# The last three experts of a hybrid decoder step keep their tokens' rows on chip and norm them there; all other rows are normed while those experts run

## Chip, cores and metric

One core of one Trainium2 chip. The metric is the device time of one execution in microseconds (us); the kernel before took 1431.51 us, the median of 3 runs (1427.43 to 1433.01).

## What is computed

One step of a one-layer trunk over 1024 prompt tokens and 32 sample tokens of width 1024, all in float32: RMSNorm, a projection, two mixers (an RWKV-7 recurrence and sliding-window attention), an output projection, and then the part that the change is in:

```python
x = x + (mixed @ prm['w_out']).astype(x.dtype)
h2 = rmsnorm(x, prm['norm_ffn_g'])
x = x + hier_moe(h2.reshape(Bn * T, D), prm).reshape(Bn, T, D).astype(x.dtype)
...
y = rmsnorm(x, norm_final_g)      # for the prompt and for the sample tokens
```

`hier_moe` sends each token to one of 4 groups (top 1) and in it to 2 of the group's 4 experts (top 2). An expert is `(silu(x @ w_gate) * (x @ w_up)) @ w_down` with 1024 x 512 and 512 x 1024 matrices, and its rows are added with the token's weight. A token's two experts always lie in one group, so experts of different groups share no token. RMSNorm multiplies a row by one over the root of its mean square (plus 1e-6) and by the gains.

## The kernel before, in words

Everything up to the routing fills the first 930 us of the profile. Then `h2` (the normed rows) and `x` lie in DRAM as `h2_dram` and `x_dram`, the second with 160 spare rows behind the 1056 tokens, and the 16 experts run one after the other, each over 160 slots: 128 in part A (`xgA`) and 32 in part B (`xgB`). A loop over rounds stands around them (7 at most, as many as the fullest expert needs); here one round runs and six are skipped, each with a few register and branch instructions.

An expert at position e takes these steps. GpSimd (POOL) gathers its rows from `h2_dram` with two indirect DMAs. TensorE (PE) turns them (`turn`, lines 1158 to 1172); ScalarE (ACT) and VectorE (DVE) copy the turned rows out of PSUM (`turned`). PE forms gate and up in four blocks of columns f = 0 to 3 (`gate_up`, 1174 to 1185) in two PSUM banks; ACT takes the SiLU of a block (`silu`, 1563), DVE multiplies (`product`, 2048), and block f of PE waits until the product of block f - 2 is done. `down` (1187 to 1204) writes 128 x 512 to banks 5 and 6 and the 32 slots of part B, cut into four column quarters on 4 x 32 partitions, to bank 7. ACT and DVE weight the three pieces (`rows_out`, 1570 and 2053), and POOL adds the rows to `x_dram` with two indirect accumulating DMAs (`scatter`, 2173). PE's order is turn(e), down(e - 1), gate_up(e).

SyncE (SP) issues all plain DMAs from one queue, in program order. The three matrices of an expert (2 MB each) go to one of two buffers; those of position e are asked for when down(e - 2) is done (line 552).

After the last expert's scatter has landed and the rounds are left, the tail runs: SP loads `x_dram` back into `X2` (nine tiles: eight of 128 tokens and one of 32; five DMAs in four pieces, `XL`, lines 557 to 560), ACT squares and sums each tile and takes the root (1598, 1600), DVE takes the reciprocal and multiplies by it and by the gains (2113, 2114) into `yo`, and SP stores the tiles (564).

Of the kernel before, what the change touches and what calls it, by code (L numbers as in the profile page):

```python
# [6 lines left out]
I32 = mybir.dt.int32  # L7
# [32 lines left out]
ROUNDS = -(-TOK // CAP)  # L40
LV = 6
# [24 lines left out]
sv_out sv_in st_in pool sr_ok sy_out sy_in st_out ys_ps ys_ok  # L66
# [3 lines left out]
fin """  # L70


def constants():
# [33 lines left out]
    return {"c_table": table.astype(np.float32), "c_level": level, "c_bias": bias.astype(np.float32),  # L107
# [9 lines left out]
def program(nc, i, o):  # L117

    ctx = ExitStack()
    with ctx:  # L120
# [136 lines left out]
        rt_ = {}  # L257
        for n, k in (("lg", 180), ("ga", 36), ("gb", 36), ("ohg", 36), ("prod", 144), ("leg", 36), ("oh1", 36), ("oh2", 36), ("OH1", 144), ("OH2", 144),
                     ("OHs", 144), ("tot", 144), ("rank", 144), ("cnt", 16), ("rk", 18), ("m", 9), ("gw", 9), ("m1", 9), ("m2", 9),
                     ("den", 9), ("mc", 1), ("nr", 1), ("cmp", 1), ("t16", 16), ("u16", 16)):  # L260
            rt_[n] = part(R0, k)
            R0 += k
# [11 lines left out]
        STEPS = 7  # L274
# [27 lines left out]
        assert R0 + 2 * NE <= ARENA  # L302

        yo = part(E0, NTT * D).rearrange("p (t d) -> p t d", t=NTT)
        x_quarters = x_dram.rearrange("r (j c) -> (r j) c", j=TQ)

# [68 lines left out]
        def _(sp):  # L375
# [163 lines left out]
            sp.wait_ge(s["h2o0"], 32 * 5)  # L539
            sp.wait_ge(s["h2o1"], 32 * 4)  # L540
            for a in range(2):
                load_expert(a, a)
            sp.wait_ge(s["n_rounds"], 1)
            rounds = sp.value_load(nround[0:1, 0:1], min_val=1, max_val=ROUNDS)
            with sp.Fori(0, ROUNDS) as r:  # L545
                with sp.If(rounds > r):  # L546
                    with sp.If(r > 0):
                        for a in range(2):
                            load_expert(a, a)
# [7 lines left out]
            x_rows = x_dram[0:SEQ].rearrange("(t p) d -> p t d", p=P)  # L557
            for n, (a, b) in enumerate(XL):
                sp.dma_start(X2[:, a:b, :], x_rows[:, a:b]).then_inc(s[f"x{n}"], 16)  # L559
            sp.dma_start(X2[0:NS, NT, :], x_dram[SEQ:TOK]).then_inc(s["x3"], 16)  # L560
            for t in range(NTT):
                sp.wait_ge(s["fin"], t + 1)
                dst = o["y_prompt"][0, t * P:(t + 1) * P, :] if t < NT else o["y_sample"].rearrange("b t d -> (b t) d")
# [1673 lines left out]
```

## Time and profile before

| | us |
|---|---|
| median of 3 runs | 1431.51 (1427.43 to 1433.01) |
| the profiled execution, its own time | 1429.26 |
| span of that execution, first to last instruction | 1427.5 |
| PE busy (matmuls) | 1297.9, 91% of the span |
| DVE, ACT, POOL busy | 460.1, 357.8, 279.7 |
| moved by DMA | 173.61 MB, 122 GB/s over the span |

The span is what the rows below divide; the execution's own time is 1.8 us longer, and its median over runs another 2.3 us. Times in the rows are microseconds from the first instruction. A busy share near 1 of PE does not say that it works at its peak.

### The profile page before, as it was taken

To read this page: it belongs to the slowest core of one execution; us is meant where nothing else is said; L and a number is where in the kernel's file an instruction comes from. 1 tells how busy PE (TensorE), PEld (TensorE's weight loads), DVE (VectorE), ACT (ScalarE), POOL (GpSimd) and SP (SyncE) were. 2 spreads that over 40 slices of the span, in tenths; PEclk is the share of its full clock that TensorE was granted. 3 is DMA by queue.
4 is the path that set the end of the run, shared out by engine and by line. 5 is a ranking of instruction groups with operands and counts; after the bars stand their busy time and mean duration, and the time that the engine had idled before them with its cause. 6 is when DMAs were issued, how large, how long until landed. Compare 5 with 4: busy or idle time off the path is not lost. (4 is left out here: it accounts for less than half of the span.)

```text
span 1427.5 us, 28133 instructions
## 1 busy us (share of the span) xinstructions
PE 1297.9 (91%) x12448; PEld 941.6 (66%) x12448; DVE 460.1 (32%) x879; ACT 357.8 (25%) x722; POOL 279.7 (20%) x159
## 2 busy tenths in 40 slices
PE   6999999988998988989799999489999999999990
PEld 4666656555666978777644454377887788788860
DVE  4103544366645555645342111511011111111113
ACT  4103444434442442333231112011011011101103
POOL 0000000011001999991000000011211211121010
PEclk9999999999999999999999999579999999999995
DMA  7312000100103000022303111917888788778817
GB/s 216 86 44 63 15 14 3 30 29 23 30 19 58 4 5 4 3 48 66 108 16 140 59 59 63 353 60 232 273 287 294 230 274 300 261 254 281 279 20 262
DMA packets 95259, 173.61 MB, mean 122 GB/s; under 512 B 19096, under 2 KB 41043, under 8 KB 94756
## 3 DMA queue, kind: packets, MB, share of 16 engines
q1 hardware_dynamic: 87476, 151.12, 31.3%
q0 software_dynamic: 7680, 20.98, 6.2%
q8 instruction: 82, 1.34, 0.4%
q14 instruction: 21, 0.17, 0.0%
HBM read 146.65 MB, written 26.44 MB: 121 GB/s over the span
## 5 line engine op out<-in xcount | busy, mean ns | idle before, releaser
L620 PE MATMUL ps<-arena 128*128 128x355 f32 x960 | 297.6, 466 | 1.9 <-issue 1.8
L1183 PEld LDWEIGHTS ps<-arena 128*128 128x128 f32 x2048 | 280.2, 191 | 6.9 <-issue 6.9
L1183 PE MATMUL ps<-arena 128*128 128x160 f32 x2048 | 284.1, 301 | 0.6 <-DVE arena L2046 0.6
L620 PEld LDWEIGHTS ps<-arena 128*128 128x128 f32 x960 | 179.7, 190 | 110.9 <-issue 13.4
L1083 PE MATMUL ps<-arena 128*128 128x512 f32 (+1 forms) x288 | 130.6, 603 | 0.7 <-DVE arena L1867 0.7
L860 PEld LDWEIGHTS ps<-arena 64*64 64x64 f32 x3584 | 110.3, 136 | 10.6 <-issue 6.1
L1197 PE MATMUL ps<-arena 128*128 128x512 f32 x256 | 114.1, 599 | 0.7 <-DVE arena L2051 0.7
L860 PE MATMUL ps<-arena 64*64 64x64 f32 x3584 | 114.3, 219 | 0.0
L2186 POOL DMA_INDIRECT arena<-h_dram,idxA x16 | 16.1, 1006 | 486.6 <-DVE idxB L2081 282.4
L2051 DVE TENSOR_TENSOR arena<-arena,ps 128x160 f32<-128x160 f32 x64 | 20.6, 321 | 265.5 <-ACT arena L1568 265.5
L1568 ACT ACTIVATE arena<-ps 128x160 f32<-128x160 f32 x64 | 19.5, 304 | 337.3 <-PE ps L1183 337.3
L1083 PEld LDWEIGHTS ps<-arena 128*128 128x128 f32 (+1 forms) x288 | 51.4, 183 | 66.5 <-issue 64.8
L2129 POOL TENSOR_TENSOR arena<-arena 128x1024 f32<-128x1024 f32 x4 | 11.4, 2854 | 377.8 <-DVE arena L1690 377.8
L1197 PEld LDWEIGHTS ps<-arena 128*128 128x128 f32 x256 | 47.3, 190 | 55.2 <-issue 53.6
L1256 ACT COPY arena<-ps 128x355 f32<-128x355 f32 x60 | 27.1, 452 | 175.0 <-PE ps L620 175.0
L2182 POOL DMA_INDIRECT x_dram<-arena,rowA x16 | 25.6, 1597 | 168.0 <-DVE arena L2060 168.0
L2058 DVE TENSOR_SCALAR arena<-ps,arena 128x512 f32<-128x512 f32 x16 | 12.0, 751 | 106.8 <-PE ps L1197 106.8
L2150 POOL TENSOR_TENSOR arena<-arena 128x1024 f32<-128x1024 f32 (+4 forms) x40 | 41.0, 1024 | 2.8
L1489 ACT COPY arena<-ps 128x512 f32<-128x512 f32 x40 | 23.4, 586 | 63.6 <-PE ps L860 63.6
L1719 DVE SCALAR_TENSOR_TENSOR arena<-ps,arena 128x1024 f32<-128x1024 f32 (+1 forms) x16 | 18.5, 1158 | 62.5 <-PE ps L699 62.5
L1805 DVE COPY_PREDICATED arena<-level,ps 128x512 f32<-128x512 uint8 x32 | 23.5, 734 | 41.6 <-PE ps L860 41.6
L1550 ACT COPY arena<-ps 128x512 f32<-128x512 f32 (+1 forms) x18 | 9.2, 553 | 109.3 <-PE ps L1144 109.3
(344 smaller groups left out, 1642.0 us busy)
## 6 DMA issues: line engine op xcount, KB each, us to landing
arena<-in_w_exp_gate SPq DMA_DIRECT2D x16, 2048.0 KB, 12.5
arena<-in_w_exp_up SPq DMA_DIRECT2D x16, 2048.0 KB, 17.4
arena<-in_w_exp_down SPq DMA_DIRECT2D x16, 2048.0 KB, 21.8
arena<-in_w_in SPq DMA_DIRECT2D x16, 512.0 KB, 3.9
arena<-in_x_prompt SPq DMA_DIRECT2D x9, 512.0 KB, 3.8
h_dram<-arena SPq DMA_DIRECT2D x8, 512.0 KB, 2.6
x_dram<-arena SPq DMA_DIRECT2D x8, 512.0 KB, 3.6
out_y_prompt<-arena SPq DMA_DIRECT2D x8, 512.0 KB, 5.9
```

The lines of the kernel that those rows point to most:

```text
L620: last = pe.matmul(ps[:, q % 2, 0:m], wr[:, n % 3, k, :], hT[:, k, a:a + m], start=(k == 0), stop=(k == KB - 1))
L860: last = pe.matmul(ps[row(e), 4 * b + bank, h * CH:(h + 1) * CH], lhs(e, h), rhs(e, h), start=True, stop=True)
L1083: return pe.matmul(ps[0:n, 4 * (t % 2) + hf, :], MX[:, b, t * P:t * P + n], wo[b][:, hf * 512:(hf + 1) * 512], start=(b == 0), stop=(b == 7))
L1183: last = pe.matmul(ps[:, 3 + f % 2, n * CAP:(n + 1) * CAP], w[a][:, k, f * P:(f + 1) * P], xgT[:, a, k, :], start=(k == 0), stop=(k == KB ...
L1197: last = pe.matmul(ps[:, 5 + n, :], eact[:, a, k, 0:P], edown[a][:, k, n * 512:(n + 1) * 512], start=(k == 0), stop=(k == 3))
L1256: act.copy(pT[:, pos, a:a + m], ps[:, q % 2, 0:m]).then_inc(s["p_ok"], 1)
L1489: act.copy(U[:, b].rearrange("p h t -> p (h t)"), ps[:, 4 * b, :]).then_inc(s["ru_ok"], 1)
L1568: act.activation(egl[:, f % 2, :], ps[:, 3 + f % 2, 0:CAP], ACT.Silu).then_inc(s["sl_ok"], 1)
L1805: dve.copy_predicated(TL[:, b], lm(lv, 0, 2 * JB), ps[:, 4 * b + 1, :].rearrange("p (h t) -> p h t", t=CH)).then_inc(s["rx_ok"], 1)
L2051: dve.tensor_tensor(eact[:, a, f, :], egl[:, f % 2, :], ps[:, 3 + f % 2, CAP:2 * CAP], ALU.mult).then_inc(s["ac_ok"], 1)
L2150: link(pool.tensor_tensor(stm[:, :, 0:m], stm[:, :, 0:m], stm[:, :, m:2 * m], ALU.add))
L2182: pool.indirect_dma_start(dst, bass.IndirectOffsetOnAxis(rows[:, e:e + 1], 0), src[:, e % 2, :], None, compute_op=ALU.add).then_inc(s[f"ys ...
```

## The change

The experts run in another order (`EO`): the first 13 positions hold experts 0 to 6, 8 to 10 and 12 to 14; the last three hold 7, 11 and 15, which lie in three groups and share no token. The first 13 add their rows to `x_dram` as before. For each of the last three, POOL gathers the `x_dram` rows of its slots (`xsA`, `xsB`), DVE adds the expert's weighted output to them on chip, and they are normed in slot order. Part B's mean square is the sum of four partitions' sums; PE forms it by a matmul with a 0/1 matrix `same` that takes the place of `strict` in the table. POOL then scatters the finished rows to both outputs by plain indirect DMAs with a bound on the index: one to `y_prompt` and one to `y_sample` for each of parts A and B, and indices outside an output are dropped.

Once the first 13 scatters have landed, the whole of `x_dram` is loaded into `X2`, squared on ACT between the SiLUs of position 14 and normed in place on DVE before and during position 15, and stored. The rows of the last three experts' tokens are written twice, the second time by the scatters, which wait until the stores have landed. The old tail is gone.

In the diff, `EO[e]` in place of `e` as an index of rows, weights and matrices, a renaming of two semaphores and the declarations are left out, as is what serves rounds after the first.

```diff
+LAST = 3
+EO = [e for e in range(NE) if e % EPG < EPG - 1 or e < EPG] + [e for e in range(EPG, NE) if e % EPG == EPG - 1]
+ACC = NE - LAST
...
+        gq = part(S0, TD)
+        xsA = [part(S0 + TD, D), xgA[:, 0, :], xgA[:, 1, :]]
+        YST = [32 * len(range(k, ACC, 2)) for k in range(2)]
+        FA, FD, FP = 22, 7, LAST
...
 # SP
+            sp.dma_start(x_dram[TOK:TOK + P, :], X2[:, 0, :]).then_inc(s["h2o0"], 16)
+            sp.dma_start(x_dram[TOK + P:, :], X2[0:XB, 1, :]).then_inc(s["h2o1"], 16)
...
-                    with sp.Fori(1, NE // 2) as q:
-                        for a in range(2):
-                            sp.wait_ge(s["ya_ps"], 3 * (NE * r + 2 * q + a) - 3)
-                            load_expert(2 * q + a, a)
+                    for e in range(2, NE):
+                        sp.wait_ge(s["ya_ps"], 3 * (NE * r + e) - 3)
+                        load_expert(EO[e], e % 2)
+                        if e == 2:
+                            sp.dma_start(same, i["c_same"]).then_inc(s["x0"], 16)
+                            for j in range(TQ):
+                                sp.dma_start(gq[j * XB:(j + 1) * XB, :], i["norm_final_g"][None, j * TD:(j + 1) * TD].to_broadcast([XB, TD])).then_inc(s["x0"], 16)
+                    for k in range(2):
+                        sp.wait_ge(s[f"yst{k}"], YST[k] * (r + 1))
+                        alone(sp)
+                    for n, (a, b) in enumerate(XL):
+                        if n == 0:
+                            sp.wait_ge(s["x0"], X_IN[0] + 80 * (r + 1) + 16 * r)
+                        sp.dma_start(X2[:, a:b, :], x_rows[:, a:b]).then_inc(s[f"x{n}"], 16)
+                    sp.dma_start(X2[0:NS, NT, :], x_dram[SEQ:TOK]).then_inc(s["x3"], 16)
+                    for t in range(NTT):
+                        sp.wait_ge(s["fin"], NTT * r + t + 1)
+                        dst = y_rows[t * P:(t + 1) * P, :] if t < NT else ys_rows
+                        sp.dma_start(dst, X2[0:toks(t), t, :]).then_inc(s[f"h2o{t % 2}"], 16)
...
 # PE
+                    def quarter_sums(k):
+                        pe.wait_ge(s["fn_act"], FA * r + (1, 15, 21)[k])
+                        pe.matmul(ps[:, 7, TD:TD + 1], same, stat[:, (50, 35, 47)[k]:(51, 36, 48)[k]], start=True, stop=True).then_inc(s["fn_pe"], 1)
+                    turn(g0 + NE - 2, 0, False)
+                    down(g0 + NE - 3, 1, False)
+                    gate_up(g0 + NE - 2, 0, False)
+                    pe.wait_ge(s["x0"], X_IN[0] + 96 * (r + 1))
+                    quarter_sums(0)
+                    turn(g0 + NE - 1, 1, False)
+                    pe.wait_ge(s["fn_act"], FA * r + 13)
+                    down(g0 + NE - 2, 0, False)
+                    gate_up(g0 + NE - 1, 1, False)
+                    quarter_sums(1)
+                    pe.wait_ge(s["fn_act"], FA * r + 17)
+                    down(g0 + NE - 1, 1, False)
+                    quarter_sums(2)
...
 # ACT: silu(g, a, first, between) calls between(f) after the SiLU of block f
+                    def rows(t):
+                        for k, (a, b) in enumerate(XL):
+                            if t == a:
+                                act.wait_ge(s[f"x{k}"], X_IN[k] + ((96, 16, 16, 32)[k]) * (r + 1))
+                        n = toks(t)
+                        if t:
+                            act.wait_ge(s["fn_act"], fa + 2 + t)
+                        square(eyA[0:n, 0, :], X2[0:n, t, :], t).then_inc(s["fn_act"], 1)
+                    def before_last(f):
+                        if f == 0:
+                            act.wait_ge(s["yo_dve"], 2 * (g0 + ACC) + 2)
+                            act.wait_ge(s["yst1"], YST[1] * (r + 1))
+                            square(eyB[:, 1, :], xsB[:, 0, :], 50).then_inc(s["fn_act"], 1)
+                            square(eyA[:, 1, :], xsA[0], 9).then_inc(s["fn_act"], 1)
+                            rows(0)
+                        elif f < 3:
+                            for t in range(3 * f - 2, 3 * f + 1):
+                                rows(t)
+                        else:
+                            rows(7)
+                            rows(8)
+                            act.wait_ge(s["fn_act"], fa + 11)
+                            root(10, stat[:, 0:10]).then_inc(s["fn_act"], 1)
+                            act.wait_ge(s["fn_pe"], FP * r + 1)
+                            root(30, ps[:, 7, TD:TD + 1]).then_inc(s["fn_act"], 1)
+                    def at_last(f):
+                        if f == 0:
+                            act.wait_ge(s["yo_dve"], 2 * (g0 + ACC + 1) + 2)
+                            act.wait_ge(s["fn_dve"], FD * r + 2)
+                            square(eyA[:, 0, :], xsA[1], 32).then_inc(s["fn_act"], 1)
+                            square(eyB[:, 0, :], xsB[:, 1, :], 35).then_inc(s["fn_act"], 1)
+                        elif f == 3:
+                            act.wait_ge(s["fn_act"], fa + 14)
+                            root(33, stat[:, 32:33]).then_inc(s["fn_act"], 1)
+                            act.wait_ge(s["fn_pe"], FP * r + 2)
+                            root(36, ps[:, 7, TD:TD + 1]).then_inc(s["fn_act"], 1)
...
 # DVE: sums(k, h) adds piece h of expert k of the last three; bulk(t) norms tile t of X2 in place; own and own_tail norm xsA and xsB
+                    dve.wait_ge(s["fn_act"], fa + 13)
+                    dve.reciprocal(stat[:, 20:30], stat[:, 10:20])
+                    again(dve.reciprocal(stat[:, 31:32], stat[:, 30:31]))
+                    own(eyA[:, 1, :], 0, 29)
+                    own_tail(eyB[:, 1, :], 0, 31)
+                    bulk(0)
+                    bulk(1)
+                    turned(g0 + NE - 1, 1)
+                    bulk(2)
+                    sums(1, 0)
+                    bulk(3)
+                    bulk(4)
+                    sums(1, 1)
+                    bulk(5)
+                    sums(1, 2)
+                    bulk(6)
+                    product(g0 + NE - 1, 1, after_last)      # bulk(7), bulk(8) after its first block
+                    dve.wait_ge(s["fn_act"], fa + 17)
...
+                    own(eyA[:, 0, :], 1, 34)
+                    own_tail(eyB[:, 0, :], 1, 37)
+                    sums(2, 0)
...
+                    sums(2, 1)
+                    sums(2, 2)
...
+                    own(X2[:, 0, :], 2, 46)
...
+                    own_tail(X2[:, 1, 0:TD], 2, 49)
...
 # POOL
+                    for k in range(2):
+                        pool.wait_ge(s[f"yst{k}"], YST[k] * (r + 1))
+                    for k in range(LAST):
+                        if k:
+                            pool.wait_ge(s["xb_ps"], NE * r + (ACC + k + 1))
+                            pool.wait_ge(s["xs_in"], 32 * LAST * r + 32 * k)
+                        gather(xsA[k], x_dram, rowA[:, e:e + 1]).then_inc(s["xs_in"], 16)
+                        gather(xsB[:, k, :], x_quarters, rowB[:, e:e + 1]).then_inc(s["xs_in"], 16)
+                    pool.wait_ge(s["h2o0"], H2O[0] + 16 * 5 * (r + 1))
+                    pool.wait_ge(s["h2o1"], H2O[1] + 16 * 4 * (r + 1))
+                    for k, (outA, outB) in enumerate(((eyA[:, 1, :], eyB[:, 1, :]), (eyA[:, 0, :], eyB[:, 0, :]), (X2[:, 0, :], X2[:, 1, 0:TD]))):
+                        pool.wait_ge(s["fn_dve"], FD * r + (1, 3, 6)[k])
+                        put(y_rows, outA, rowA[:, e:e + 1], SEQ - 1)
+                        put(ys_rows, outA, smpA[:, k:k + 1], NS - 1)
+                        pool.wait_ge(s["fn_dve"], FD * r + (2, 4, 7)[k])
+                        put(y_quarters, outB, rowB[:, e:e + 1], TQ * SEQ - 1)
+                        put(ys_quarters, outB, smpB[:, k:k + 1], TQ * NS - 1)
```

The last write of each expert is its own `put`; `round_done` waits for all of them. Before the experts, DVE forms the sample indices `smpA` and `smpB` by six short instructions between the first gathers' release and the first scatter's.

## Rows read from the trace of the kernel before

**Rows 1.** The page: busy time by engine, in all.
```profile
PE 1297.9 (91%) x12448; PEld 941.6 (66%) x12448; DVE 460.1 (32%) x879; ACT 357.8 (25%) x722; POOL 279.7 (20%) x159
```

**Rows 2.** Timeline, position 15 and the tail: start, us, engine, line, operation [idle before].
```profile
1361.94 17.65 PE L1183 MATMUL ps<-arena 128*128 128x160 f32 x128
...
1380.34 7.13 PE L1197 MATMUL ps<-arena 128*128 128x512 f32 x16 [0.75 <-DVE arena L2051]
...
1387.40 1.93 PE L1202 MATMUL ps<-arena 128*32 128x256 f32 x32
...
1389.41 0.49 DVE L2060 TENSOR_SCALAR arena<-ps,arena 128x256 f32<-128x256 f32 x1 [1.14 <-PE ps L1202]
1390.75 1.55 POOL L2182 DMA_INDIRECT x_dram<-arena,rowA  x1 [23.97 <-DVE arena L2060]
1392.60 1.55 POOL L2182 DMA_INDIRECT x_dram<-arena,rowB  x1 [0.30 <-issue]
1400.80 1.95 SPq L559 DMA_DIRECT2D arena<-x_dram  x4
1401.53 1.28 ACT L1592 ACT_TABLE_LOAD   x1 [16.77 <-issue]
...
1402.83 0.20 ACT L1592 ACTIVATE stat<-eps 128x1 f32<-128x1 f32 x1
...
1405.96 0.16 DVE L2113 RECIPROCAL stat<-stat 128x1 f32<-128x1 f32 x1 [16.07 <-ACT stat L1600]
1406.16 1.28 DVE L2114 SCALAR_TENSOR_TENSOR arena<-arena,stat 128x1024 f32<-128x1024 f32 x1
...
1409.95 1.04 ACT L1598 ACTIVATE arena<-arena 128x1024 f32<-128x1024 f32 x1
...
1410.89 0.18 ACT L1598 ACTIVATION_READ_ACCUMULATOR arena<-arena 128x1 f32 x1
1411.11 0.29 ACT L1600 ACTIVATE stat<-stat,eps 128x1 f32<-128x1 f32 x1
```

**Rows 3.** Timeline, position 14 (gate_up from 1333.94), with SP's and POOL's issues.
```profile
1307.40 1.60 POOL L2182 DMA_INDIRECT x_dram<-arena,rowA  x1 [7.30 <-DVE arena L2060]
...
1333.94 17.65 PE L1183 MATMUL ps<-arena 128*128 128x160 f32 x128
...
1334.22 0.37 SPq L534 DMA_DIRECT2D arena<-in_w_exp_gate  x1
...
1335.31 7.58 SPq L534 DMA_DIRECT2D arena<-in_w_exp_down  x1
...
1347.28 0.30 ACT L1568 ACTIVATE arena<-ps 128x160 f32<-128x160 f32 x1 [4.04 <-PE ps L1183]
1347.62 0.32 DVE L2051 TENSOR_TENSOR arena<-arena,ps 128x160 f32<-128x160 f32 x1 [4.03 <-ACT arena L1568]
...
1353.01 7.13 PE L1197 MATMUL ps<-arena 128*128 128x512 f32 x16
```

**Rows 4.** Windows: PE, PEld, DVE, ACT, POOL busy (count), PEclk, DMA share, GB/s.
```profile
896.00:928.00 32.00, 15.59 (x156) 12.06 (x156) 18.97 (x87) 1.49 (x2) 0.00 (x0) 0.50 1.03 388
1334.90:1356.20 21.30, 21.30 (x147) 19.42 (x147) 1.71 (x5) 2.29 (x6) 3.11 (x2) 1.00 1.00 324
...
1356.00:1357.00 1.00, 1.00 (x4) 0.40 (x3) 0.00 (x0) 0.25 (x1) 0.00 (x0) 1.00 0.19 74
...
1406.00:1407.00 1.00, 0.00 (x0) 0.00 (x0) 0.96 (x2) 0.00 (x0) 0.00 (x0) 0.50 1.01 397
```

**Rows 5.** Windows as in rows 4, around a fall and a rise of the granted clock.
```profile
943.00:944.00 1.00, 1.00 (x7) 1.00 (x6) 0.00 (x0) 0.00 (x0) 0.00 (x0) 0.66 0.93 377
...
1394.00:1395.00 1.00, 0.00 (x0) 0.00 (x0) 0.00 (x0) 0.00 (x0) 0.15 (x1) 0.61 1.05 193
```

**Rows 6.** Chain that ended last: start, us, what; the last scatter and the loads.
```profile
1392.60 4.89 DMA x_dram<-arena,rowB
...
1402.79 13.97 DMA arena<-x_dram
```

**Rows 7.** DMA issues: issuer, count, size, median us from issue to landing.
```profile
arena<-in_w_exp_down SPq DMA_DIRECT2D x16, 2048.0 KB, 21.8
...
arena<-h_dram,idxB POOLq DMA_INDIRECT x16, 3.8
x_dram<-arena,rowA POOLq DMA_INDIRECT x16, 9.8
```

**Rows 8.** Timeline around the first expert: gathers, first turn, first gate_up.
```profile
934.11 0.96 POOL L2186 DMA_INDIRECT arena<-h_dram,idxA  x1 [0.30 <-issue]
935.38 0.86 POOL L2186 DMA_INDIRECT arena<-h_dram,idxB  x1 [0.30 <-issue]
936.76 1.97 PE L1165 MATMUL ps<-table,arena 128*128 128x128 f32 x8 [6.52 <-DMA arena<-h_dram,idxB]
...
940.32 3.03 PE L1183 MATMUL ps<-arena 128*128 128x160 f32 x10 [0.60 <-DVE arena L2046]
```

More of the change, by code:

```diff
@@ L554, in _ @@
+                    sp.wait_ge(s["h2o0"], H2O[0] + 16 * 5 * (r + 1))
+                    alone(sp)
+                    sp.wait_ge(s["h2o1"], H2O[1] + 16 * 4 * (r + 1))
+                    alone(sp)
                     sp.wait_ge(s["round_done"], r + 1)
                     alone(sp)
[L557 to L560, printed above, removed]
@@ L1582, in _, with square, root @@
                     g0 = NE * r
+                    fa = FA * r
+                    def square(dst, src, col):
+                        return act.activation(dst, src, ACT.Square, accum_out=stat[0:dst.shape[0], col:col + 1])
+                    def root(dst, src, bias=1):
+                        return act.activation(stat[:, dst:dst + (10 if dst == 10 else 1)], src, ACT.Sqrt, scale=1.0 / D, bias=eps[:, 0:1] if bias else stat[:, 44:45])
+                    def rows(t):
[6 more added lines that the diff above has]
+                        square(eyA[0:n, 0, :], X2[0:n, t, :], t).then_inc(s["fn_act"], 1)
@@ new lines, in _ @@
+                    act.wait_ge(s["h2o0"], H2O[0] + 16 * 5 * (r + 1))
+                    act.wait_ge(s["yo_act"], g0 + NE)
+                    square(X2[:, 2, 0:512], xsA[2][:, 0:512], 42).then_inc(s["fn_act"], 1)
+                    act.wait_ge(s["yo_dve"], 2 * (g0 + NE) - 1)
+                    square(X2[:, 2, 512:], xsA[2][:, 512:], 43).then_inc(s["fn_act"], 1)
+                    act.wait_ge(s["fn_act"], fa + 19)
+                    act.wait_ge(s["fn_dve"], FD * r + 5)
+                    root(45, stat[:, 43:44], 0).then_inc(s["fn_act"], 1)
@@ L1589, in _ @@
+                    act.wait_ge(s["yo_dve"], 2 * (g0 + NE))
+                    square(X2[:, 4, 0:TD], xsB[:, 2, :], 47).then_inc(s["fn_act"], 1)
+                    act.wait_ge(s["fn_pe"], FP * r + 3)
+                    root(48, ps[:, 7, TD:TD + 1]).then_inc(s["fn_act"], 1)
                     act.wait_ge(s["round_done"], r + 1)
                     alone(act)
-            act.activation(stat[:, 40:41], eps[:, 0:1], ACT.Sqrt)
-            for t in range(NTT):
-                n = toks(t)
-                for k, (a, b) in enumerate(XL):
-                    if t == a:
-                        act.wait_ge(s[f"x{k}"], X_IN[k] + 16 + 16 * (k == 3))
-                act.activation(sqj3[0:n, :], X2[0:n, t, :], ACT.Square, accum_out=stat[0:n, t:t + 1]).then_inc(s["sumsq"], 1)
-                act.wait_ge(s["sumsq"], 2 * NTT + t + 1)
-                act.activation(stat[0:n, 10 + t:11 + t], stat[0:n, t:t + 1], ACT.Sqrt, scale=1.0 / D, bias=eps[0:n, 0:1]).then_inc(s["std_ok"], 1)
@@ L2104, in _ @@
+                    own(X2[:, 0, :], 2, 46)
+                    dve.wait_ge(s["fn_act"], fa + 22)
+                    again(dve.reciprocal(stat[:, 49:50], stat[:, 48:49]))
+                    own_tail(X2[:, 1, 0:TD], 2, 49)
                     assert steps[0] == STEPS
@@ L2193, in _ @@
                 with pool.If(rounds > r):
+                    with pool.If(r > 0):
+                        for k in range(LAST):
+                            e = EO[ACC + k]
+                            put(x_dram, xsA[k], rowA[:, e:e + 1], TOK - 1)
+                            put(x_quarters, xsB[:, k, :], rowB[:, e:e + 1], TQ * TOK - 1)
+                        pool.wait_ge(s["fo_out"], 96 * LAST * r)
+                        alone(pool)
                     pool.wait_ge(s["i_ok"], r + 1)
```

175 lines of the change are left out of this document (115 added, 60 removed).

## The prediction, as put on record before the change was run

> **What bounds the kernel now.** I read the page's busy times first: PE is busy for 91% of the span [rows 1]. The reader is to see that any time in which PE waits inside the experts is paid in full. Then the timeline of the last expert: gate_up runs from 1361.94 to 1379.6, down's last matmul ends at 1387.40 + 1.93 = 1389.3, and from there to the span's end at 1427.5 stand 38.2 us in which PE does nothing [rows 2]. The chain of waits says what they are: the last scatter, until 1397.5, the six skipped rounds until SP's loads at 1400.8, the way of `x_dram` back until 1416.8, and the last tiles' norm and stores [rows 2, 6]. The change wants these 38.2 us. The windows show the other resource: while an expert's matrices flow, the 16 DMA engines are full (share 1.00 from 1334.9 to 1356.2), and from 1356.2 on they are nearly empty [rows 4].
>
> **The order on SP's queue.** The reload of `x_dram` now stands behind the load of position 15 on SP. That load is asked for when down(13) is done, at 1334.2, and its last issue ends at 1335.31 + 7.58 = 1342.9 [rows 3], though the 13th expert's scatters are issued from 1307.4 on [rows 3] and have landed some 12 us later. So the nine tiles flow behind 6 MB of matrices, and ACT waits for the first of them after the first SiLU of position 14, a quarter into gate_up, at about 1338.4. This wait I follow.
>
> **When the tiles land.** Before, the matrices take 21.3 us at 324 GB/s beside position 13's two accumulating scatters [rows 4], which the change removes. A scatter alone fills the engines as well: it takes 4.89 us to land with nothing beside it [rows 6], 9.8 beside matrices [rows 7]. The matrices of positions 0 and 1 flow without scatters at 388 GB/s [rows 4]; 6.29 MB at that rate are 16.2 us, from about 1335.3 to 1351.5. The other bound is that nothing is won: 1356.2. I take the first, since its row has no scatter either. `X2` is 1056 rows of 4 KB, 4.33 MB; at 397 GB/s, the rate of the old reload [rows 4], 10.9 us. In the order of the queue, with 0.9 us until the slowest engine has landed (21.8 us after 1335.31 is 1357.1, against 1356.2 of the windows [rows 7, 4]): tile 0 at 1353.7, tiles 1 and 2 at 1356.4, 3 to 5 at 1360.3, the rest at 1363.3.
>
> **ACT in position 14.** A square with its accumulator is 1.04 + 0.18 and overlaps to 1.16 us a tile (1409.95 to 1411.11) [rows 2]. Tile 0 until 1354.9, second SiLU and product 0.30 + 0.32 and two hops [rows 3]: 1355.7. Block 3 of gate_up needs that product; it stood ready at 1347.3, so PE stands still for 8.4 us. ACT goes on: tiles 1 and 2, tile 3 until 1361.5, SiLU, tiles 4 to 6 until 1365.3, SiLU, tiles 7 and 8 until 1368.0, table load 1.28, root 0.29 [rows 2], small root 0.2: 1369.8. PE has meanwhile done block 3 (4.4, and 1.7 lost to the clock, below) and turn(15) (1.4 to 1.6: 1351.6 to 1353.0 before), by 1363.5, and waits for `fn_act` 13 ahead of down(14), which was at 1353.0 before [rows 3]. **Delay of PE: 16.8 us.** Queued behind this wait are down(14), gate_up(15) and all after them; DVE and the stores wait for the same count.
>
> **The clock.** The granted clock stood at 2.4 GHz until about 1394.2, 4.9 us after PE's last matmul, and then at 1.2 [rows 5, 2]. PE rests here for 8.4 and 6.3 us, so I take both restarts at 1.2 GHz. At 940.32 gate_up began at the low level and got the high one at about 943.7, 3.4 us later [rows 8, 5]. Of the second restart half of that is lost, 1.7 us, on the path; the first is hidden, since ACT is still waiting for tiles. Bounds: nothing, or 3.4 if it stays low as long as after 936.76 (6.9 us) [rows 8, 5].
>
> **Between gate_up(15) and down(15).** Before, 0.75 us [rows 2]. Now SiLU 0.30, table load 1.28, root 0.29, the small root 0.2 and hops: 2.25. **1.5 us more.** DVE's nine tiles of 1.28 [rows 2], one own tile with its part B and the three `sums` of position 14 make 16 us from 1370 on. turned(15) comes after five of them, at 1375, before gate_up(15) at 1380.6, and the rest fits into its 17.65. The stores end by 1393. These I cost at nothing; their cover is gate_up(15), and without it they would cost 10 us.
>
> What the Trainium skill has against the change, apart from the sum: its page "ScalarE: Activation LUTs" (Table sets: the hidden batching unit) asks for all calls of one table before the next is loaded, and prices a switch at about 2.66 us, drain included. The change puts Sqrt between SiLUs: two such switches lie on the path. The row has 1.28 and the next activation 0.02 us after it [rows 2], which speaks against the drain here; by the page's price the result would be 2.8 us higher, an estimate.
>
> **The new tail.** From PE's last matmul: `sums(2, 2)` 0.1 + 0.49; reciprocal and own row norm until 2.1 [rows 2] (the root of part A comes earlier, part B's beside it); hop to POOL 0.85 (1389.90 to 1390.75); three more issues at 1.86, the spacing of the two scatters: 5.6; landing 4.89 [rows 2, 6]; skipped rounds 3.2 (1397.5 to 1400.8 [rows 6, 2]); end 0.4. **Sum 17.1 us** in place of 38.2. The plain bounded scatter is in no row. From below: a gather's spacing of 1.27 (934.11 to 935.38) and 3.8 to land [rows 8, 7], 3 us less; from above: twice the 1.55 of an accumulating issue, 3.1, in the second rival. I take the scatter's own row, the nearest.
>
> **The rest.** Three pairs of gathers replace three of scatters and hide under gate_up. Two stores (0.64 MB, 1.6 us at 397 GB/s) precede the first matrices on SP; those of position 0 are there long before gate_up(0) at 940.3, which waits for gathers and copies [rows 8]. The six short DVE instructions fall before turn(0) is done at 938.7 [rows 8]. PE's unrolled code I take as free, its loop being only the same instructions. All at nothing; if the cover fails, 2 us.
>
> **Sum:** 16.8 + 1.7 + 1.5 + 17.1 - 38.2 = -1.1 us on the span of 1427.5, the execution of 1429.26. That execution lies 2.3 us under the median, 1431.51; by the same difference the changed kernel has 1430.4, I say **1430.5 us**. The tail's gain is real, but the tiles that were to hide behind experts stop PE for nearly as long.
>
> **Rivals.** (1) PE isn't held: the tiles are there in time, as the order of the code suggests. Then 38.2 - 17.1 - 1.5 = 19.6 us are won: 1412. Against it, whatever the order on the queue, 6.29 + 4.33 MB from 1334.2 on need 27 us at 388 GB/s, and all nine squares stand ahead of down(14). Chance 0.06.
> (2) POOL's bounded scatters become the tail. Twelve stand in its queue, the first four from 1393 on, the last four not before 1412.3. At 1.86 us each there is room; from 2.4 us on the second four push the last. At 3.1: 1405.4, 1417.8, last issue at 1427.1, landed 1432.0, end 1435.7, 8.2 us over the span: 1440. For it: a bound and indices to drop are more work than any row shows. Against: the accumulating ones need only 1.55. Chance 0.17.
> (3) The matrices flow no faster without scatters: everything 4.7 us later, 1435, still no change that can be told. Chance 0.17.
> (4) The forecast, 0.60. That the change doesn't overlap as it says is thus the forecast itself: the pass over `X2` runs in PE's standstill.
>
> **The numbers.** About 0.5%, 7 us, is what a measurement of this kernel can tell from no change. Low end: cheap scatters (-3), no cold restart (-1.7), tiles 2 us earlier: 1424. High end: rival 2, or rival 3 with the longer restart and slow scatters: 1441. Faster by over 0.5% takes rival 1 and the low edge of the forecast: 0.13. Slower takes rival 2 and parts of 3 and 4: 0.23. The rest, 0.64, is within.
>
> **What would show it.** Right: SP's issues of the reload right after 1343; PE idle before block 3 of position 14, released by DVE behind an ACT that waited for DMA, and again before down(14), released by ACT, together 15 us; granted clock 0.5 in both restarts; the last matmul at about 1409; some 17 us behind it. Wrong: PE without gaps, or the gap elsewhere; a tile landing before 1352; POOL issues above 2.4 us; a tail over 22 us.

## The result, and the profile after

The changed kernel took **1440.22 us**, the median of 4 runs (1437.84 to 1443.76), beside 1431.9 us of the kernel before in 4 runs of the same chip: a ratio of 1.0066 with a 95% interval of 1.0036 to 1.0096. In a second set of runs, 8 of it beside 25 of the kernel before, it was 1438.54 against 1432.72, 1.0049 (1.0026 to 1.0072). It is slower by about half a per cent: the medians lie 8.3 and 5.8 us apart, and both intervals lie above 1. (The ratio is of the means of the runs.) The forecast was 1430.5, no change that can be told. The time lies inside the range, near its high end, but the time did change, and for the worse.

The profiled execution took 1437.84 us, its span is 1436.0, against the 1427.5 of before. Busy times of the page, then the two costliest groups of PE (busy us, mean ns of one | idle before them, what ended most of it):

```profile
PE 1305.8 (91%) x12454; PEld 944.6 (66%) x12454; DVE 467.1 (33%) x893; ACT 361.6 (25%) x731; POOL 288.0 (20%) x171
...
L1218 PE MATMUL ps<-arena 128*128 128x160 f32 x2048 | 285.6, 302 | 10.3 <-DVE arena L2158 9.7
...
L1232 PE MATMUL ps<-arena 128*128 128x512 f32 x256 | 117.1, 611 | 8.4 <-ACT stat L1643 8.4
```

PE has six matmuls more (its three small sums for part B, at some 0.3 us each) and 7.9 us more of busy time [rows 1]: for the most part a slower clock, not more work. Beside it new waits stand in the experts, one of 9.7 us ended by DVE and two, together 8.4 us, ended by ACT's root (line 1643). The timeline places them (start, us, engine, line, operation [idle before]):

```profile
1338.66 13.31 PE L1218 MATMUL ps<-arena 128*128 128x160 f32 x96
1338.79 0.37 SPq L558 DMA_DIRECT2D arena<-in_w_exp_gate  x1
...
1339.82 4.25 SPq L558 DMA_DIRECT2D arena<-in_w_exp_down  x1
...
1344.64 7.86 SPq L589 DMA_DIRECT2D arena<-x_dram  x4
...
1359.92 1.06 ACT L1640 ACTIVATE arena<-arena 128x1024 f32<-128x1024 f32 x1 [14.79 <-DMA arena<-x_dram]
...
1361.66 6.05 PE L1218 MATMUL ps<-arena 128*128 128x160 f32 x32 [9.70 <-DVE arena L2158]
...
1373.56 1.28 ACT L1643 ACT_TABLE_LOAD   x1
1374.85 0.30 ACT L1643 ACTIVATE stat<-stat,eps 128x10 f32<-128x10 f32 x1
...
1375.54 10.17 PE L1232 MATMUL ps<-arena 128*128 128x512 f32 x16 [6.16 <-ACT stat L1643]
...
1387.50 17.65 PE L1218 MATMUL ps<-arena 128*128 128x160 f32 x128
...
1407.48 7.10 PE L1232 MATMUL ps<-arena 128*128 128x512 f32 x16 [2.22 <-ACT stat L1643]
...
1414.52 1.93 PE L1237 MATMUL ps<-arena 128*32 128x256 f32 x32
...
1419.46 0.98 POOL L2362 DMA_INDIRECT out_y_prompt<-arena,rowA  x1 [4.91 <-DVE arena L2238]
1420.75 0.98 POOL L2362 DMA_INDIRECT out_y_sample<-arena,smpA  x1 [0.30 <-issue]
1422.04 0.99 POOL L2362 DMA_INDIRECT out_y_prompt<-arena,rowB  x1 [0.31 <-issue]
1423.33 0.99 POOL L2362 DMA_INDIRECT out_y_sample<-arena,smpB  x1 [0.30 <-issue]
```

The reader is to see the forecast's chain in it. SP issues the reload at 1344.64, behind position 15's matrices. ACT stands still for 14.79 us until the first tile is there at 1359.92. PE waits before block 3 of gate_up(14), then before down(14), and once more before down(15). The last matmul ends at 1416.45; before it was 1389.33 [rows 2]. From there to the span's end are 19.55 us, in place of 38.17.

The windows of the same kernel (PE, PEld, DVE, ACT, POOL busy (count), PEclk, DMA share, GB/s):

```profile
1352.00:1356.00 4.00, 0.00 (x0) 0.00 (x0) 0.00 (x0) 0.00 (x0) 0.00 (x0) 0.80 1.03 410
1371.00:1372.00 1.00, 0.00 (x0) 0.00 (x0) 0.32 (x1) 1.00 (x4) 0.69 (x2) 0.73 0.28 33
1375.00:1376.00 1.00, 0.46 (x1) 0.49 (x2) 0.63 (x3) 1.00 (x4) 0.00 (x0) 0.50 0.00 0
1381.00:1382.00 1.00, 1.00 (x2) 0.35 (x2) 0.20 (x1) 0.00 (x0) 0.00 (x0) 0.65 0.92 373
```

PE rests and the DMA engines are full (share 1.03): here the last matrices and `X2` flow. The granted clock falls within the first rest, about 2.4 us after PE's last matmul (0.80 over the window's 4 us puts the fall at 1354.4), and again within the second. down(14) starts at 1.2 GHz and has 2.4 GHz again at about 1381.7. That costs it 10.17 - 7.13 = 3.04 us.

**What ends the span** is in rows that stand for no arithmetic: the sequencers' instructions at the close of the program (line, engine's sequencer, operation: ns min/median/max, first and last start in us), and PE's for the rounds that are skipped.

```profile
L124 POOLq DRAIN  x1: 6277/6277/6277, 1429.4 to 1429.4; - x1
...
L124 PEldq DRAIN  x1: 8/8/8, 1433.7 to 1433.7; - x1
```

```profile
L1243 PEldq COMPARE_BRANCH  x7: 86/224/3391, 1425.8 to 1433.6; - x7
```

The last put has landed at about 1425.5 (issue 1423.33, 2.1 us to land). POOL then walks through six skipped rounds until 1429.4 and drains for 6.28 us, to 1435.7; the span ends at 1436.0. PE needs until 1433.7 for the same skipped rounds, with one branch of 3.4 us. In the kernel before the same two pieces exist and cost nothing, because the old tail runs beside them:

```profile
L120 POOLq DRAIN  x1: 5295/5295/5295, 1401.5 to 1401.5; - x1
L120 PEldq DRAIN  x1: 8/8/8, 1406.2 to 1406.2; - x1
...
L120 SPq DRAIN  x1: 13/13/13, 1427.2 to 1427.2; - x1
```

**Where the 8.5 us of the two spans lie.** Down(12), still ahead of all new waits, starts at 1301.73 in place of 1297.01. The first line is of the changed kernel, the second of the kernel before:

```profile
1301.73 7.13 PE L1232 MATMUL ps<-arena 128*128 128x512 f32 x16
...
1297.01 7.13 PE L1197 MATMUL ps<-arena 128*128 128x512 f32 x16
```

So 4.7 us are lost before anything that the change was forecast to cost. Then comes the delay of down(14), 17.8 us (1375.54 - 4.72 - 1353.01), its slow clock 3.0, the gap between gate_up(15)'s end at 1405.15 and down(15) 2.33 - 0.75 = 1.6; the tail gives back 38.17 - 19.55 = 18.6. The sum is 4.7 + 17.8 + 3.0 + 1.6 - 18.6 = 8.5.

### The profile page after: what moved, and what is told of

It is laid out like the page before. It is cut to its first block, busy times and chain, and to the rows that moved or that the text cites. A ratio compares the mean times of both kernels' runs of the same rounds, so it can differ in the third digit from the quotient of the medians.

```text
span 1436.0 us, 28214 instructions
## 1 busy us (share of the span) xinstructions
PE 1305.8 (91%) x12454; PEld 944.6 (66%) x12454; DVE 467.1 (33%) x893; ACT 361.6 (25%) x731; POOL 288.0 (20%) x171
## 4 chain that ended last, share of the span: by engine, by line
PE 84%; DVE 6%; issue 4%; ACT 2%; DMA 2%; SPq 1%; POOL 0%; DVEq 0%; ACTq 0%; POOLq 0%
PE ps L655 19%; PE ps L1218 18%; PE ps L1118 8%; PE ps L1232 8%; PE ps L895 7%; PE ps L1237 2%; PE ps L734 2%; PE ps L757 2%; DMA arena<-x_dram 1%; PE ps L1185 1%; PE ps L747 1%; PE ps L928 1%; PE ps L1200 1%; PE ps L694 1%; PE ps L1249 1%
## 5 line engine op out<-in xcount | busy, mean ns | idle before, releaser
L655 PE MATMUL ps<-arena 128*128 128x355 f32 x960 | 301.6, 471 | 2.8 <-issue 2.6
L1218 PEld LDWEIGHTS ps<-arena 128*128 128x128 f32 x2048 | 281.5, 192 | 16.8 <-DVE arena L2158 9.9
L1232 PE MATMUL ps<-arena 128*128 128x512 f32 x256 | 117.1, 611 | 8.4 <-ACT stat L1643 8.4
L895 PEld LDWEIGHTS ps<-arena 64*64 64x64 f32 x3584 | 110.5, 136 | 10.6 <-issue 6.1
L2358 POOL DMA_INDIRECT x_dram<-arena,rowA x13 | 20.9, 1606 | 95.3 <-DVE arena L2168 95.3
```

Source lines behind the costliest of these rows:

```text
L655: last = pe.matmul(ps[:, q % 2, 0:m], wr[:, n % 3, k, :], hT[:, k, a:a + m], start=(k == 0), stop=(k == KB - 1))
L895: last = pe.matmul(ps[row(e), 4 * b + bank, h * CH:(h + 1) * CH], lhs(e, h), rhs(e, h), start=True, stop=True)
L1218: last = pe.matmul(ps[:, 3 + f % 2, n * CAP:(n + 1) * CAP], w[a][:, k, f * P:(f + 1) * P], xgT[:, a, k, :], start=(k == 0), stop=(k == KB ...
L1232: last = pe.matmul(ps[:, 5 + n, :], eact[:, a, k, 0:P], edown[a][:, k, n * 512:(n + 1) * 512], start=(k == 0), stop=(k == 3))
```

## The experiments

All times are medians in us; the ratio is to the kernel before, run beside it on the same chip. The variants ran on three chips, on which the kernel before had 1432.17, 1432.41 and 1432.72. "Rest" is taken from the one profiled execution: its span less the start of gate_up(0), so that it leaves out what happens ahead of the experts. It still holds gate_up(0), which takes 19.0 to 20.7 us with the granted clock of its execution, so rests differ by up to 1.6 us for that alone. "Tail" is from the end of the last matmul to the span's end.

| kernel | median (runs) | ratio, 95% interval | gate_up(0) | rest | tail |
|---|---|---|---|---|---|
| before | 1431.9 to 1432.7 | 1 | 940.3 | 487.1 | 38.2 |
| changed | 1440.22 (4) | 1.0066 (1.0036 to 1.0096) | 945.2 | 490.7 | 19.6 |
| after_again | 1438.54 (8) | 1.0049 (1.0026 to 1.0072) | 946.3 | 491.1 | 19.5 |
| reload_first | 1424.24 (6) | 0.9939 (0.9914 to 0.9964) | 948.9 | 476.7 | 19.5 |
| squares_late | 1437.57 (10) | 1.0033 (1.0015 to 1.0052) | 944.0 | 493.5 | 19.5 |
| cell | 1430.74 (10) | 0.9993 (0.9971 to 1.0014) | 945.6 | 484.2 | 19.5 |
| first_cell | 1414.81 (4) | 0.9888 (0.9856 to 0.9919) | 944.2 | 468.5 | 19.6 |
| rounds_dyn | 1432.49 (10) | 1.0001 (0.998 to 1.0022) | 943.2 | 490.2 | 15.9 |
| before_dyn | 1429.6 (10) | 0.9977 (0.996 to 0.9993) | 941.0 | 482.0 | 33.1 |
| before_head | 1432.2 (12) | 1.0012 (0.9994 to 1.0029) | 940.8 | 486.4 | 37.6 |
| after_drain | 1438.16 (10) | 1.0047 (1.0024 to 1.0071) | 937.8 | 491.6 | 18.0 |
| dyn_drain | 1428.09 (10) | 0.9969 (0.9947 to 0.9992) | 940.8 | 483.8 | 10.6 |
| first_cell_dyn | 1413.02 (4) | 0.9881 (0.9849 to 0.9912) | 940.1 | 465.3 | 15.8 |
| first_cell_dyn_drain | 1407.06 (6) | 0.9831 (0.9806 to 0.9857) | 943.7 | 460.4 | 11.1 |

### 1. reload_first: the reload ahead of position 15's matrices

```diff
                     for e in range(2, NE):
+                        if e == NE - 1:
+                            (waits for yst0, yst1; the five loads of X2)
                         sp.wait_ge(s["ya_ps"], 3 * (NE * r + e) - 3)
                         load_expert(EO[e], e % 2)
```

> SP issues the reload of x_dram ahead of position 15's matrices; nothing else is changed. Theory (the reload stands behind 6 MB on SP's queue, and ACT and PE wait for it): the tiles land beside the first half of position 14 or earlier, the 9.7 us gap before block 3 goes, the 6.2 us gap before down(14) shrinks to some 3 us (ACT still has nine squares, a table load and two roots between its SiLUs), down(14) is back at 7.13 us from 10.17, and the median is 17 us under the changed kernel's 1440.2: 1422 to 1425, ratio to the kernel before 0.993 to 0.995. Rival (bytes, not order: the matrices of position 15 are now late by the reload's 11 us and PE waits for them instead): a gap of 5 to 10 us before gate_up(15), 1430 to 1437.

Measured: 1424.24, 0.9939, 14 to 16 us under the changed kernel. Its timeline:

```profile
1327.18 5.91 SPq L583 DMA_DIRECT2D arena<-x_dram  x4
...
1342.36 17.65 PE L1219 MATMUL ps<-arena 128*128 128x160 f32 x128
...
1364.57 8.80 PE L1233 MATMUL ps<-arena 128*128 128x512 f32 x16 [2.90 <-ACT stat L1644]
...
1395.43 8.80 PE L1233 MATMUL ps<-arena 128*128 128x512 f32 x16 [2.50 <-ACT stat L1644]
```

The reload is issued 15 us before the matrices (those at 1342.49), gate_up(14) runs in one piece of 17.65 us, and the wait before down(14) shrinks from 6.16 to 2.90. Down(14) starts 59.1 us after down(12) (1305.43) in place of 73.8, against 56.0 in the kernel before: the order on SP's queue was the cause of 14.7 of the 17.8 us of delay. The median came as expected. Down(14) had been expected back at 7.13, though, and both downs still lose 8.80 - 7.13 = 1.7 us to the clock, behind rests of only 2.9 and 2.5 us.

### 2. squares_late: the same late tiles, but not ahead of the SiLUs

```diff
-                            rows(0)
-                        elif f < 3:
-                            for t in range(3 * f - 2, 3 * f + 1):
+                        elif f == 3:
+                            for t in range(7):
                                 rows(t)
-                        else:
```

> ACT squares all nine tiles behind the last SiLU of position 14 instead of between its SiLUs; the reload stays behind the matrices. Theory (only the wait ahead of down(14) is on the path, the gap before block 3 is hidden in it): block 3 follows block 2 without a gap, the gap before down(14) grows to some 16 us, and the time stays within 2 us of the changed kernel's 1440.2. Rival (each gap is paid): 8 to 10 us less, 1430 to 1432.

```profile
1339.03 17.66 PE L1218 MATMUL ps<-arena 128*128 128x160 f32 x128
...
1376.22 9.12 PE L1232 MATMUL ps<-arena 128*128 128x512 f32 x16 [12.39 <-ACT stat L1643]
```

The 9.7 us before block 3 are gone, and down(14) waits 12.39 us in place of 6.16. The median of 1437.57 is 1 to 3 us under the changed kernel's, the rest of the one profile 2.6 us over its own (about 1.5 of them in gate_up(0), which took 20.67 us in place of 19.11). The median is 2.6 us under 1440.2, just outside the 2 us expected, and the gap before down(14) was put at some 16 us; but the rival's 8 to 10 us are not there, with 9.7 us of standstill gone. Down(14) starts 74.1 us after down(12), against 73.8 in the changed kernel. Of the two gaps only the second one counted, as expected: it is the last tile that lets down(14) go, and where PE waits for it doesn't matter.

### 3. cell: the wait of down itself

PE waits for `fn_act` 13 and 17 because the small sum of part B sits in bank 7, which down needs. Here it sits in a free cell of bank 2, and both waits go.

```diff
-                        pe.matmul(ps[:, 7, TD:TD + 1], same, ...)
+                        pe.matmul(ps[:, 2, KB * XB:KB * XB + 1], same, ...)
...
-                    quarter_sums(0)
                     turn(g0 + NE - 1, 1, False)
-                    pe.wait_ge(s["fn_act"], FA * r + 13)
+                    quarter_sums(0)
                     down(g0 + NE - 2, 0, False)
...
-                    pe.wait_ge(s["fn_act"], FA * r + 17)
```

> The changed kernel with part B's sums in a cell of PSUM bank 2 that neither turn nor down writes; PE's two waits for ACT's roots (fn_act 13 ahead of down(14), 17 ahead of down(15)) fall away, the reload stays late. Theory: down(14) follows turn(15) at once and runs during ACT's squares; gate_up(15) now waits for DVE, which does five tiles and the copy of the turned rows after fn_act 13, so it starts about 5 us after fn_act 13 instead of 12: 7 us less, and 2 to 3 us less before down(15) with the clock: median 1429 to 1432. Rival (the squares, not PE's wait, are what is paid, so the wait only moves): within 2 us of 1440.2.

```profile
1362.21 6.31 PE L1218 MATMUL ps<-arena 128*128 128x160 f32 x32 [9.54 <-DVE arena L2156]
...
1372.29 8.83 PE L1232 MATMUL ps<-arena 128*128 128x512 f32 x16 [1.97 <-DVE arena L2156]
...
1401.31 7.13 PE L1232 MATMUL ps<-arena 128*128 128x512 f32 x16 [0.63 <-DVE arena L2156]
```

Down(14) still waits 1.97 us, now for its own products behind the same late squares, and down(15) waits 0.63 us and runs at the high clock. Gate_up(15) follows down(14) at once; it had been expected to wait for DVE. 6.7 us are won in the rest (490.9 in the mean of the two profiles of the changed kernel, against 484.2), and 8 to 9.5 in the median.

### 4. first_cell: both

The edits of reload_first and cell together.

> reload_first and cell together. In reload_first PE still stood 2.9 us before down(14) and 2.5 before down(15), and both downs took 8.8 us instead of 7.13 since the clock fell in those gaps. Theory: both gaps go to under 1 us and both downs to 7.13: 7 to 8 us under reload_first's 1424.2, so 1416 to 1417, ratio to before 0.989. Rival (the short waits are no reason of the low clock, or DVE's tiles then hold gate_up(15)): only 3 us less, 1421.

```profile
1356.93 7.11 PE L1233 MATMUL ps<-arena 128*128 128x512 f32 x16
...
1384.25 7.13 PE L1233 MATMUL ps<-arena 128*128 128x512 f32 x16 [0.64 <-DVE arena L2157]
```

1414.81, 0.9888: PE rests in the last experts no longer than in the kernel before (0.64 us before down(15), there 0.75), and neither down loses to the clock. The rest is 22.4 us under the mean of the changed kernel's two profiles. The three terms that the prediction charged to PE measure 17.8 + 3.0 + 1.6, 22.4 us in all: this amount.

### 5. rounds_dyn and before_dyn: no skipped rounds

```diff
-            with pe.Fori(0, ROUNDS) as r:
+            with pe.Fori(0, rounds) as r:
```

and the same on the four other engines, in the changed kernel and in the kernel before.

> The changed kernel with the loop over rounds ended at the number of rounds that the data need, on all five engines, so that no round is skipped. Theory (the span's last 10 us are the engines' way through six skipped rounds, PE's the longest with 8.1 us): 8 us less, 1432, and the span ends 2 to 3 us after the last scatter has landed. Rival (the end is the last scatter or the closing of the program, and PE's branches lie beside it): within 2 us of 1440.2.

> The kernel before with the same loop. Theory (there only SP's skipped rounds, 3.2 us, stood between the last scatter and the reload; PE's 8.4 us lay beside the old tail): 3 us less, 1428.5 to 1429.5, ratio 0.998. Rival (PE's were paid too): 8 us less, ratio 0.994; or nothing: 1.000.

rounds_dyn took 1432.49, 6 to 8 us less than the changed kernel. Of this its profile puts 3.7 us at the end (the tail falls from 19.55 to 15.86), since POOL's drain still closes the span:

```profile
L124 POOLq DRAIN  x1: 6275/6275/6275, 1427.0 to 1427.0; - x1
...
L124 PEldq DRAIN  x1: 8/8/8, 1427.1 to 1427.1; - x1
```

The median came where it was expected, but not by the reason given: PE's skipped rounds, which lasted until 1433.7, were not what ended the program. What is won is POOL's share of them, 3.9 us, and the 8 us expected are not in the profile. In the kernel before the same edit wins 5.1 us of tail (38.17 to 33.12) but some 3 in the median. The profile of rounds_dyn gives a part of its gain back (rest 490.2): it has a slow down(15) as well, 1.7 us, which the profiled execution of the changed kernel has not. Neither median is explained to the microsecond by its single profile.

### 6. after_again and after_drain, dyn_drain: POOL's closing drain

The kernel again, and with one instruction more: POOL drains its queue early, behind its last gathers and ahead of the puts, where it waits anyhow.

```diff
+                    pool.drain()
                     pool.wait_ge(s["h2o0"], H2O[0] + 16 * 5 * (r + 1))
```

> The changed kernel itself, in more runs, since its first median (1440.2) is from 4. If that median was a good one: 1439 to 1441, ratio 1.0045 to 1.0065. From the profiles alone (34.1 us tail and stalls worked out against the same part of before, without the early part): span from the first gate_up 490.7 against 487.1, so 3.6 us more than before: 1436, ratio 1.0025. A value between tells that a part of the 8 us was the chance of few runs.

> The changed kernel with one drain of POOL ahead of the finished rows' scatters, where POOL waits for the stores anyway. The closing of the program drains POOL: 6.28 us in every profile of the changed kernel, with 76 indirect DMAs, 5.30 in those of the kernel before, with 64. Theory (the drain costs some 82 ns for each indirect DMA since the last drain, and in the changed kernel it is the last thing of the span): the early drain takes about 5.8 us hidden, the closing one about 1 us; then PE's skipped rounds end last, 2 us earlier than now: 1.9 us less than after_again. Rival (the closing drain has a fixed cost): 6.3 us again, nothing gained.

> after_drain with the loop ended at the number of rounds needed. Theory: both hidden costs are off the end: the span ends 1.5 to 2 us after the last scatter has landed, against 10.5 in the changed kernel: 8 to 9 us less than after_again. Rival (fixed drain): 3.7 us less.

after_again took 1438.54, so that a part of the first 8.3 us may be the chance of four runs. The closing drain falls to 1.04 us in after_drain, and there PE's skipped rounds become what ends the span:

```profile
L124 POOLq DRAIN  x1: 1040/1040/1040, 1424.4 to 1424.4; - x1
...
L124 PEldq DRAIN  x1: 8/8/8, 1429.2 to 1429.2; - x1
```

The early drain itself, and the last gather ahead of it:

```profile
L2402 POOLq DRAIN  x1: 7449/7449/7449, 1365.3 to 1365.3; - x1
...
1366.29 0.95 POOL L2365 DMA_INDIRECT arena<-x_dram,rowB  x1 [0.30 <-issue]
```

The tail is 18.0 in place of 19.5, and the median (1438.16 against 1438.54) does not move by what can be told. With both edits, dyn_drain, the tail is 10.63 and the median 1428.09, 10 us under the changed kernel and under the kernel before as well (0.9969). Two hidden pieces lay beside each other, so that taking away either one alone shows the other: alone they won 3.7 and 1.5 us of tail, together 8.9.

### 7. before_head: what the change adds ahead of the experts

The kernel before with the changed kernel's two extra stores, its semaphores, two tiles and its constant, and nothing else of it.

```diff
+            sp.dma_start(x_dram[TOK:TOK + P, :], X2[:, 0, :]).then_inc(s["h2o0"], 16)
+            sp.dma_start(x_dram[TOK + P:, :], X2[0:XB, 1, :]).then_inc(s["h2o1"], 16)
...
+            link(dve.memset(stat[:, NT:NTT], 1.0))
```

> The kernel before with only what the change does ahead of the experts: the two stores to the spare rows, the six-word additions to SBUF, the renamed semaphores, the added input, one memset. Question: the profile of the changed kernel stands 4.7 us later than the one of before already at position 12, and all of it lies ahead of the routing, where nothing was changed. Theory A (chance of the clock in one profile): ratio to the kernel before 0.999 to 1.001. Theory B (the additions shift the part ahead of the routing): 3 to 5 us more, ratio 1.002 to 1.0035.

1432.2 against 1432.17, 1.0012 (0.9994 to 1.0029): these additions cost nothing that 12 runs beside 23 can tell, though the interval still reaches up to 4 us and so into theory B. A part of what makes gate_up(0) late is seen in the trace as clock. The first window is of the changed kernel, the second of the kernel before, the third of reload_first, whose code up to there is the changed kernel's:

```profile
170.00:180.00 10.00, 10.00 (x44) 6.35 (x43) 6.66 (x9) 4.09 (x13) 0.00 (x0) 0.84 0.18 52
```

```profile
170.00:180.00 10.00, 10.00 (x49) 6.51 (x48) 6.67 (x9) 3.59 (x12) 0.00 (x0) 1.00 0.18 52
```

```profile
170.00:180.00 10.00, 10.00 (x45) 6.34 (x44) 6.67 (x9) 4.28 (x14) 0.00 (x0) 0.85 0.18 52
```

PE is busy throughout in all three, and in two of them the granted clock is 0.84 and 0.85 for this stretch, some 3 us of it at the low level, with 44 and 45 matmuls done in place of 49. Over the eleven profiles of kernels with the changed kernel's head, gate_up(0) begins anywhere from 937.8 to 948.9, with no edit there to explain it. Up to gate_up(0) PE is busy for 852.2 us in the changed kernel and for 849.6 before: 2.6 of the 4.9 us are PE's own work done more slowly, and the other 2.3 are idle time of PE, whose cause stays open. The mean start over the eleven is 943.6, though, against 940.3 to 941.0 in the three profiles of kernels made from the one before. Whether the changed kernel's head is a few us slower in the mean isn't settled by three profiles, and before_head can't settle it for what it leaves out. The six short instructions on DVE are not it: from the cast of `idxA` to gate_up(0) pass 9.97 us in the changed kernel (935.24 to 945.21) and 10.01 before (930.31 to 940.32).

### 8. The version that beats both

first_cell_dyn adds the round loop of experiment 5 to first_cell; first_cell_dyn_drain adds the early drain too.

> first_cell with the loop over rounds ended at the number of rounds needed. If the parts add up: 8 us less than first_cell, 1408 to 1409, ratio to before 0.983 to 0.984. If the skipped rounds overlap with something that now ends last: less than half of that.

> All four together: the reload ahead of position 15's matrices, the cell in bank 2, the loop ended at the rounds needed, the early drain. Theory: 5 us under first_cell_dyn, so 1406 to 1408 in the median, ratio to before 0.982 to 0.984. Rival (fixed drain): as first_cell_dyn, 1411 to 1413.

first_cell_dyn took 1413.02, which its interval does not separate from first_cell's 1414.81; in the profile the tail is 3.7 us shorter and the rest as a whole 3.2. The 8 us that it would have won if the parts had added up did not come: POOL's drain still closes the span. All four edits give **1407.06 us, 0.9831 (0.9806 to 0.9857)**: 1.7% under the kernel before, over 2% under the changed one. The end of its timeline and its closing drain:

```profile
1365.64 17.65 PE L1219 MATMUL ps<-arena 128*128 128x160 f32 x128 [0.18 <-DMA arena<-in_w_exp_down]
...
1391.10 1.93 PE L1238 MATMUL ps<-arena 128*32 128x256 f32 x32
...
1400.36 0.99 POOL L2361 DMA_INDIRECT out_y_sample<-arena,smpB  x1 [0.30 <-issue]
```

```profile
L124 POOLq DRAIN  x1: 1037/1037/1037, 1402.8 to 1402.8; - x1
```

The first line shows the next bound: gate_up(15) waits 0.18 us for the last of its matrices to land, since they now flow behind `X2`. These 0.18 us are all that a still earlier reload could win there.

## Why the prediction was right and wrong

**In short.** The forecast of no change failed. The mechanism held: PE stands still in position 14, and that gives the tail's gain back. What failed first is a step of the new tail, "skipped rounds 3.2 (1397.5 to 1400.8 [rows 6, 2]); end 0.4": 3.6 us from the last landing to the end, where the profile has 10.5. It is 6.9 us short; cheaper puts gave 4.4 of them back. The clock's term was 1.3 us short and the delay 1.0. That 1440 lies inside the range is luck in part: its high end was reckoned with slow puts, and the puts were cheap. In the profile 4.7 us more, the late start of the experts, were in no term.

**The reload behind the matrices: right.** This was the argument on which the forecast stood against rival 1, and reload_first shows it by undoing it. The other argument against rival 1, that 10.6 MB from 1334.2 on need 27 us "whatever the order on the queue", does not hold: with the reload first its bytes start 15 us before the matrices, and first_cell, with both waits gone, comes to 1414.81, near that rival's 1412. Tile 0 was there 21.1 us after SP had asked for the matrices (1338.79 to 1359.92), where 19.5 was worked out. At 388 GB/s 1.6 us too many were hoped for: the removed scatters gave back about 3 of the 4.7 us that the two bounds left open, so the truth lay between forecast and rival 3, nearer the forecast.

**The delay of down(14): 16.8 forecast, 17.8 measured.** Both gaps came where they were put, 9.70 and 6.16 us in place of 8.4 and 6.3, and that only the second one counts was borne out by squares_late.

**The clock: mis-sized.** "Of the second restart half of that is lost, 1.7 us" was 3.04 in this execution, inside the bounds. Over the five profiles that keep both gaps and waits (changed, after_again, rounds_dyn, after_drain, dyn_drain) down(14) lost 3.0, 1.4, 2.9, 2.1 and 2.8 us. And one restart was left out: the gap before down(15) was charged at 1.5 us (1.6 measured), but in four of those five the clock fell in it too, and down(15) took 8.75 to 8.80 in place of 7.13, 1.6 to 1.7 us more. The profile of the changed kernel is the one of the five in which it did not.

**The table switches.** The trace has 1.28 us for each of the loads on the path and the next activation right behind (1373.56 to 1374.85), as in the kernel before. The higher price, by which 2.8 us would have been added (the Trainium skill, "ScalarE: Activation LUTs"), isn't borne out, and cell shows how the switch leaves the path altogether: down need not wait for the root.

**The new tail: its two halves were both wrong, in opposite ways.** The failed step's 3.2 us were SP's, the engine that went on first in the old tail. In the changed kernel nothing follows the skipped rounds that could cover the other engines: from the landing of the last put to the end are 10.5 us, POOL's skipped rounds 3.9, its drain 6.28 and 0.3 besides. The drain stood in the trace of before, 5.30 us long at 1401.5, and hidden; it was not in the sum. That is 6.9 us too little. On the other side the puts were cheaper than "three more issues at 1.86" and "landing 4.89": the spacing is 1.29, and they land after 2.1 us (shortest; median 2.4, longest 3.4), so that from the last matmul to the last landing 9.05 us passed where 13.4 were counted, 4.4 us too much. The lower bound, taken from the gathers, was the nearer neighbour: the puts are issued at a gather's spacing (1.29 and 1.27), and land sooner than its 3.8. Rival 2, which needed issues above 2.4 us, is thereby refuted.

**Together.** Leaving the head out, the profile has +3.8 us (17.8 + 3.0 + 1.6 - 18.6) where the forecast had -1.1. The difference of 4.9 is the tail 2.5, the delay 1.0, the clock 1.3 and the gap 0.1. The head of that execution adds 4.7. The medians stand 5.8 and 8.3 us apart. Some 4 of that is found in the rests of the profiles (490.7 and 491.1 against 487.1 and 486.4); what remains, the second restart before down(15) among it, varies with the clock from one execution to the next, and a small cost of the head stays possible. The statement that the tail's gain is given back by PE's standstill held: 18.6 won, 22.4 lost, and those 22.4 came back whole when first_cell took both causes away.

## What to carry over

When a tail is removed, list what every engine still has to do after the last useful instruction, also what the old tail covers: skipped loop rounds and closing drains stand in the sequencers' rows, and each becomes the bound once its cover is gone. When a pass is moved under other work, ask first what stands ahead of its loads in the queue, and whether the wait that it adds protects data or only a shared PSUM cell. Two ends that lie side by side show nothing when only one is cut; try both together before giving either up.

## What was not expected of the hardware

- POOL's drain costs by the indirect DMAs issued since the last one: 5.295 us behind 64, 6.277 behind 76, 1.04 behind 12. (6.277 - 5.295) / 12 is 82 ns each; 12 and 64 times that are 0.98 and 5.2 us. The early drain, also behind 64, is recorded with 7.4 us in after_drain and dyn_drain, where nothing waits for it, but it starts while the last two gathers are still being issued: from their end (1367.24) to its own (1372.75) are 5.5 us, which fits.
- The granted clock fell in rests of PE of only 2 to 2.9 us or in the first half microsecond behind them (reload_first: 2.90 and 2.50; after_drain: 2.34; cell: 1.97, with down(14) at 8.83), each with 1.7 us lost in the 16 matmuls behind. It isn't the length alone: after the same 2.22 us down(15) took 7.10 in the changed kernel's profile and 8.75 in after_again's.
- A bounded scatter that only writes is issued every 1.29 us and lands after 2.4; the accumulating one stands at 1.85 and 4.89 to 9.8 [rows 2, 6, 7].
- A skipped round is not free: in the changed kernel PE needs 8.2 us for six (1425.5 to 1433.7), with one branch of 3.4 us; POOL 3.9.
